# Attention masks: identity products on TensorE, or an add by VectorE in PSUM

## What is computed

```python
valid = (jnp.abs(qpos[:, :, None] - kpos[:, None, :]) <= WINDOW) & ((kpos >= 0) & (kpos < L))[:, None, :]
s_loc = jnp.where(valid[None, :, None, None], s_loc, -jnp.inf)
m = jnp.maximum(jnp.maximum(jnp.max(s_loc, axis=-1, keepdims=True), jnp.max(s_ctx, axis=-1, keepdims=True)), sink_b)
p_loc = jnp.exp(s_loc - m)
```

## Time and profile before

| | |
|---|---|
| Median of 3 runs | 1461.41 us (1461.40 to 1462.18) |
| Profiled execution | 1462.61 us |
| Its span, first to last instruction | 1460.8 us |
| TensorE busy, matmuls | 1432.5 us, 98% |
| TensorE busy, weight loads | 1315.9 us, 90% |
| VectorE busy | 882.0 us, 60% |
| ScalarE busy | 659.3 us, 45% |
| GpSimd busy | 120.1 us, 8% |

### The profile page before, as it was taken

How to read it: one execution, slowest core, us unless ns; L and a number is a source line. 1 busy time by engine, 2 the same in 40 slices (tenths; PEclk the granted TensorE clock), 3 DMA queues, 4 the chain that set the end, 5 groups by cost and what they waited for, 6 DMA issues and landing times.

```text
span 1460.8 us, 21008 instructions
## 1 busy us (share of the span) xinstructions
PE 1432.5 (98%) x8329; PEld 1315.9 (90%) x8329; DVE 882.0 (60%) x1465; ACT 659.3 (45%) x1166; POOL 120.1 (8%) x118
## 2 busy tenths in 40 slices
PE   5999999999999999999999999999999999999998
PEld 2899788878899999999988997889889999999998
DVE  3686656665466645455656975567646675556563
ACT  3656554333635525243537575542436453434352
POOL 1000203230001000000010011031300010000000
PEclk9999999999999999999999999999999999999999
DMA  9566425444434766766436432323343434344341
GB/s 337 178 200 191 130 73 159 146 145 143 139 107 154 234 210 210 233 215 204 128 90 182 126 107 67 101 73 116 84 118 116 126 119 130 118 128 129 118 130 44
DMA packets 187336, 210.27 MB, mean 144 GB/s; under 512 B 10798, under 2 KB 156006, under 8 KB 187238
## 3 DMA queue, kind: packets, MB, share of 16 engines
q1 hardware_dynamic: 187238, 208.93, 46.1%
HBM read 204.97 MB, written 3.93 MB: 143 GB/s over the span
## 4 chain that ended last, share of the span: by engine, by line
PE 88%; DVE 6%; ACT 2%; DMA 1%; issue 1%; SPq 1%; ACTq 0%; DVEq 0%
PE bank L681 23%; PE bank L682 23%; PE bank L683 23%; PE bank L697 3%; PE bank L698 3%; PE bank L699 3%; DVE tb L1638 2%; DMA raw<-in_w_mod_dram 1%; PE y_ps L935 1%; DVE wlo L1520 1%; PE bank L719 1%; PE seg_ps L719 1%; PE y_ps L836 1%; PE y_ps L966 1%; PE seg_ps L820 1%
## 5 line engine op out<-in xcount | busy, mean ns | idle before, releaser
L1520 DVE TENSOR_TENSOR wlo<-raw,whi 128x1024 fp32r<-128x1024 f32 (+1 forms) x288 | 352.2, 1230 | 234.5 <-ACT whi L1109 233.3
L681 PE MATMUL bank<-ahi,whi 128*128 128x384 f32 (+1 forms) x1280 | 442.9, 346 | 0.4 <-DVE wlo L1520 0.4
L682 PE MATMUL bank<-alo,whi 128*128 128x384 f32 (+1 forms) x1280 | 433.1, 338 | 0.0
L683 PE MATMUL bank<-ahi,wlo 128*128 128x384 f32 (+1 forms) x1280 | 433.0, 338 | 0.0
L1109 ACT CAST whi<-raw 128x1024 fp32r<-128x1024 f32 (+1 forms) x288 | 296.1, 1035 | 302.5 <-PE bank L683 178.0
L681 PE MATMUL bank<-bhi,whi 128*128 128x384 f32 x768 | 263.6, 343 | 0.0
L682 PE MATMUL bank<-blo,whi 128*128 128x384 f32 x768 | 259.4, 338 | 0.0
L683 PE MATMUL bank<-bhi,wlo 128*128 128x384 f32 x768 | 259.4, 338 | 0.0
L681 PEld LDWEIGHTS bank<-ahi,whi 128*128 128x128 f32 x1280 | 241.5, 189 | 11.6 <-issue 8.6
L682 PEld LDWEIGHTS bank<-alo,whi 128*128 128x128 f32 x1280 | 241.7, 189 | 3.0 <-issue 2.4
L683 PEld LDWEIGHTS bank<-ahi,wlo 128*128 128x128 f32 x1280 | 241.3, 189 | 0.0
(11 more groups left out here) (250 smaller groups left out, 1371.6 us busy)
## 6 DMA issues: line engine op xcount, KB each, us to landing
raw<-in_w_mlp_dram SPq DMA_DIRECT2D x128, 512.0 KB, 3.7
raw<-in_w_in_dram SPq DMA_DIRECT2D x104, 512.0 KB, 3.9
raw<-in_w_mod_dram SPq DMA_DIRECT2D x84, 512.0 KB, 6.3
raw<-in_w_ssd_o_dram SPq DMA_DIRECT2D x16, 512.0 KB, 3.5
raw<-in_w_out_dram SPq DMA_DIRECT2D x16, 512.0 KB, 3.4
raw<-in_w_pool_o_dram SPq DMA_DIRECT2D x8, 512.0 KB, 3.6
raw<-in_w_attn_o_dram SPq DMA_DIRECT2D x8, 512.0 KB, 3.6
arena_s<-in_w_mod_dram SPq DMA_DIRECT2D x6, 512.0 KB, 4.6
```

The costliest lines, as they stand in the source:

```text
L681: nc.tensor.matmul(dst, uh[:, k, tm_cols(m)], hi[k0 + k], start=first and k == 0, stop=False)
L682: nc.tensor.matmul(dst, uh[:, k, tm_cols(m)], lo[k0 + k], start=False, stop=False)
L683: ins = nc.tensor.matmul(dst, ul[:, k, tm_cols(m)], hi[k0 + k], start=False, stop=last and k == 3)
L1520: nc.vector.tensor_tensor(rest, full, top.bitcast(F32), ALU.subtract).then_inc(lo_ready, 1)
```

## The change

`head_max` gets one instruction ahead of its reduction, for masked pairs: VectorE adds the triangle to 128 columns of both heads' scores in `seg_ps`, in place, and the reduction waits for it. The mask products of `scores(i)` go, so that its last score matmul signals `scores_ready`. With them go the tile `mask_r`, its three copies by ScalarE at the start, and the semaphore `tri_ready` that TensorE waited for. The triangles are read from the constants as they were loaded.

```diff
-        mask_r = sb("mask_r", [P, 3, P], F32R)
+        masks = (const("mask1"), const("mask2"))
...
-            pe.wait_ge(tri_ready, 3)
...
                     for h in range(2):
                         part = slice(64 * h, 64 * h + 64)
                         ins = nc.tensor.matmul(seg_ps[:, h, 0:b - a], qT[part, hp, tm_cols(t)], kT[part, hp // 2, a:b],
-                                               start=True, stop=t == 0)
-                    if t:
-                        at = P if t == 1 else 0
-                        for h in range(2):
-                            ins = nc.tensor.matmul(seg_ps[:, h, at:at + P], mask_r[:, 0, :], mask_r[:, t, :], start=False,
-                                                   stop=True)
+                                               start=True, stop=True)
                     ins.then_inc(scores_ready, 1)
...
-            for n, name in enumerate(("ident", "mask1", "mask2")):
-                nc.scalar.copy(mask_r[:, n, :], const(name)).then_inc(tri_ready, 1)
...
                     dve.wait_ge(scores_ready, l * 12 + i + 1)
+                    if t:
+                        at = P if t == 1 else 0
+                        own = seg_ps[:, :, at:at + P]
+                        link(nc.vector.tensor_tensor(own, own, masks[t - 1].unsqueeze(1).to_broadcast([P, 2, P]), ALU.add))
                     link(nc.vector.tensor_reduce(nmax, seg_ps[:, :, 0:n], AX_X, ALU.max, negate=True))
```

More of the change, by code:

```diff
@@ L379, in backbone_step @@
                                                                sem("column_loaded"))
-        tri_ready, ctrans, csil_ready, c4_ready = (sem("tri_ready"), sem("ctrans"), sem("csil_ready"),
-                                                              sem("c4_ready"))
+        ctrans, csil_ready, c4_ready = sem("ctrans"), sem("csil_ready"), sem("c4_ready")
         xtrans, pads_zeroed = sem("xtrans"), sem("pads_zeroed")
```

## The result

The changed kernel takes 1466.54 us (median of 6 runs, 1464.72 to 1467.82), the kernel before 1461.41: 5.1 us or 0.36% slower, ratio 1.0036, 95% interval 1.0024 to 1.0048. The forecast was 1466.5 us, slower. Times are medians; one of the seven runs of e5 took 1561.58 us at a granted clock of 0.85, and it is left out of e5's ratio.

What follows compares the result with a forecast made beforehand. TensorE, though 98% busy, was taken to wait for VectorE in five of twelve attention rounds; adds delay each layer 2.56 us, 2 x 2.56 = +5.1 us, giving 1466.5 us from 1461.41, range 1463.6 to 1469.6.

Steps and rivals of the forecast that it cites:

- T2 to T6: Starts of the probability transposes in attention rounds 2 to 6 of a layer's 0 to 11; TensorE said to wait there.
- Rival 4: The VectorE add is dear, at the 512-column price: 8.9 us in all, 1470.3 us; chance 0.12.
- a = 0.45: Delay in us of everything behind the add on VectorE: 0.42 for the add, 0.03 until the reduction follows.
- Start, first layer: Round 0's transposes: reduction 0.09 us later, less 0.23 for pair 1's removed masks, so they move by -0.14 us.
- Start, second layer: Second layer's round 0: counted like the first layer, within 0.2 us for its first reduction, which waits for a split.
- T1 joins, +0.17: Round 1's transposes: VectorE's line 1748 comes +0.31 us later with 0.14 in hand, so they move by +0.17 us.
- The GpSimd collision at T2: Round 2: normalising, lengthened by GpSimd's window sums, moves with line 1748; transposes shift +0.76 us, without the collision +0.62.
- the list of signs: What the profile after should show, including gaps before the transposes of rounds 2 to 6 wider by 0.6 to 0.7 us each.
- Nothing behind T6 gives it back: From round 7 on no mask remains and TensorE ends last; nothing there takes the first layer's +2.56 us delay back.
- Removing the products: TensorE's mask products: 0.23 us less a masked pair, sixteen pairs worth 3.7 us where TensorE ends last.
- Rival 1: VectorE is not what the transposes wait for and the add hides: 1457.7 us, faster; chance 0.05.
- Rival 3: The wait behind the add is free: 0.34 us instead of 0.45 for each add, 1465.0 us; chance 0.05.

Runs made afterwards that it cites:

- e5: The kernel before, masks still by TensorE, with attn_rest(i - 1) moved ahead of head_max(i + 1) on VectorE: 1457.69 us against 1461.52.
- e4: The changed kernel with attn_rest(i - 1) moved ahead of head_max(i + 1) on VectorE: 1454.25 us against 1461.55 for the kernel before.
- e6: The kernel before, mask products kept, plus a VectorE add written to an unused SBUF tile that nothing waits for: 1465.81 us against 1461.52.
- e2: The kernel before, mask products kept, with the waited VectorE add on top: 1467.96 us against 1461.55.
- e7: The changed kernel measured again beside the kernel before on the same chip: 1466.16 us against 1461.52, ratio 1.0032.
- e1: The changed kernel without its add, so no mask is applied at all: 1459.99 us against 1461.55 for the kernel before.

## Why the prediction was right, point by point

- *TensorE waits in T2 to T6 for line 1748.* Shown by e5: with that line moved, every gap is 0.18 us, and before gains 3.8 us (3.6 forecast). In e4 every gap but T2's is a plain handover.
- *The add, 0.42 us.* It takes 424 ns. That VectorE writes PSUM costs 6 ns: with the result in SBUF (e6) it is 418. The line through the earlier trace rows holds for this operation too. Rival 4 falls.
- *a = 0.45.* Measured 0.46 to 0.47 a round, and 0.48 once in e2; the reduction behind the add is 8 ns longer (958 for 950), the add 4 ns, which makes most of the difference.
- *Start, first layer.* T0 at -0.12 for -0.14 (-0.11 in e7).
- *Start, second layer.* Counted like the first, within 0.2 us. T0 came at -0.26, inside that, but not for the reason given; that the forecast fits here is luck. There GpSimd's window sums run at the same time, and the tiny operation behind the reduction (line 1731) ends only when GpSimd's second one does; an earlier or later reduction only changes how long it takes. Timeline of before, of after and of e2:

```profile
874.54 2.66 POOL L2037 TENSOR_TENSOR arena_s<-arena_s 128x405 f32<-128x405 f32 x2
...
876.59 0.62 DVE L1731 SCALAR_TENSOR_TENSOR small<-small 128x2 f32<-128x2 f32 x1
```
```profile
875.16 2.66 POOL L2032 TENSOR_TENSOR arena_s<-arena_s 128x405 f32<-128x405 f32 x2
...
877.54 0.30 DVE L1726 SCALAR_TENSOR_TENSOR small<-small 128x2 f32<-128x2 f32 x1
```
```profile
875.65 2.66 POOL L2042 TENSOR_TENSOR arena_s<-arena_s 128x405 f32<-128x405 f32 x2
...
878.19 0.16 DVE L1736 SCALAR_TENSOR_TENSOR small<-small 128x2 f32<-128x2 f32 x1
```

  The operation takes 0.62, 0.30 and 0.16 us and ends near GpSimd's end in the first two (877.21 and 877.20; 877.84 and 877.82). In before, after, e1, e4, e5, e6 and e7 it takes 0.29 to 0.77 us and ends 0.01 to 0.02 us behind GpSimd's. From the first scores of the layer to its end it is 2.93, 2.90 and 2.94 us in these three kernels, so the add and the earlier reduction do not count in this T0, and only the removed products of pair 1 do (0.23 us). That is why e2's add is not felt in the second T0 (+0.01, expected +0.45) and e1's gain is small there (-0.24, expected -0.59). For after it is worth 0.1 us, for e1, e2 and e6 0.35 to 0.45: the term of the expectations that was furthest off.
- *T1 joins, +0.17.* +0.19, and its gap is 0.71 us where -0.37 for TensorE and +0.17 give 0.18 + 0.54 = 0.72.
- *The GpSimd collision at T2.* T2 - T1 is 0.61 us, a round's 0.46 and 0.15 more; forecast 0.59. The gap there widened by 0.81 us, where the list of signs said 0.6 to 0.7 for each of T2 to T6. The prediction's own sum gives 0.82 for T2 (0.59, and 0.23 by which TensorE comes earlier), so the list was at odds with it there; the other four are 0.67 to 0.70. In after, round 2, as the earlier trace rows:

```profile
167.77 2.89 POOL L2032 TENSOR_TENSOR arena_s<-arena_s 128x405 f32<-128x405 f32 x3
```
```profile
169.82 1.39 DVE L1737 TENSOR_SCALAR arena_s<-arena_s,small 128x384 f32<-128x384 f32 x2
```

  The first of the two normalising operations takes 1.06 us and ends 0.21 behind GpSimd (170.88 and 170.67); the second takes 0.41, as in other rounds.
- *Nothing behind T6 gives it back.* T11 keeps T6's shift to 0.01 us in after, and T7 to T11 keep it to 0.04 in every kernel.
- *Removing the products.* 0.23 us a pair forecast; where TensorE decides, T0 to T1 of e4 shows 0.21 and 0.22.
- *The three copies of ScalarE, counted as nothing.* No run takes them out alone. In the profiles the first scores of the first layer come between 0.59 us earlier and 0.72 later than in before; after lies at -0.38 and its repeat e7 at +0.58. A gain under 1 us would not show in that.
- *Rival 1*, with the Trainium skill's rule (Perfetto Trace Analysis, section Identifying the Most-Contended Engine): weight loads are busy 90% in both kernels, and less TensorE work made the kernel slower. Taken over the whole span, the trace doesn't agree with it. Between e5 and e4, where the waits are gone from these rounds but for e4's T2, taking the same products off TensorE does gain time, 2.6 us by the traces, and there the trace agrees.
- *Rival 3*, with the Trainium skill's rule that a semaphore between VectorE operations costs nothing extra (VectorE: DVE Perf Modes, section The DRAIN you can't avoid): in e6 against e2 it costs 0.12 to 0.13 us, so the trace doesn't agree. The reduction starts 0.03 us behind the end of an add that it waits for, and 0.09 before the end of one that it doesn't.

## What to carry to other kernels

An engine that is 98% busy over the span can still wait in the very rounds that a change touches. Look at the gap between its last matmul and the next group, and at who ends it, before counting removed work as time. Where a VectorE queue sets the pace, ask first whether what the other engine waits for must stand behind what it doesn't need: one swapped pair of calls was worth 3.8 us here, and it turned a 5 us loss of the same change into a gain of some 3.

## What the runs showed of the hardware that I had not expected

- The profiled execution of before has 3.4 us at half TensorE clock (0.50 granted, 1.2 of 2.4 GHz) in the middle of work, at 319.8 us, 2.1 us behind the end of an idle of 0.9 us of TensorE, which after has too. None of the eight later profiles has the low stretch there. (All nine have another at half clock, 6.8 us long, from 36.5 to 43.3 us in before.) Before in that stretch, then after around the same work (width, then busy us of TensorE, its weight loads, VectorE, ScalarE, GpSimd, then the granted clock, the share of the DMA engines and GB/s):

```profile
319.80:323.20 3.40, 3.40 (x8) 1.57 (x7) 1.10 (x1) 0.00 (x0) 1.85 (x2) 0.50 0.06 19
```
```profile
317.00:332.00 15.00, 14.08 (x79) 12.28 (x78) 11.08 (x13) 2.86 (x4) 4.55 (x5) 1.00 0.27 71
```

  The two matmuls of 128x512 behind the idle take 1.73 us in before (from 319.53) and 1.08 in after (from 321.78). Past it, before is 1.6 us late against each of the others. This closes the account: 5.2 at the two T11, less 1.6, less the 0.4 us by which the first scores come earlier in after, gives the 3.2 us between the two profiled spans. In after the first load of x lands 0.36 us earlier, and the early stretch at half clock ends 0.52 us earlier (42.82 and 43.34). Over the nine profiles the first scores go with both: in e2 the load lands 0.37 us later than in before, but that stretch ends 1.78 us earlier, and the first scores come 0.59 us earlier. How the 0.4 divides between the two was not tested. The spread of 3 us over runs of one kernel fits with it in part: among the 15 runs of before beside e1 to e4, the six with a mean granted clock of 0.996 take 1462.5 to 1463.9 us, the nine with 0.998 or 0.999 take 1460.2 to 1461.7. Among the 13 beside e5 to e7 the one with 0.996 is the slowest too, at 1463.9, but two with 0.998 take 1462.5 and 1462.9. Those runs show only the mean clock, and what sets it off in some executions was not tested.
- A VectorE operation of two numbers a partition can last four times as long (0.62 us for 0.16) while GpSimd works on SBUF. The Trainium skill (SBUF — State Buffer, section Who interferes with whom) has the rule: an operation of VectorE with two SBUF inputs contends with GpSimd's reads, and of one in a two-port mode and GpSimd's the later has to wait until the first is done. The rows agree: the operation at the second layer's start has two SBUF inputs and ends 0.01 to 0.02 us behind GpSimd's, and the first normalising operation of round 2 ends 0.21 us behind. No run took GpSimd's work away, so that the ends go together is what is shown.
